# A two-layer model on one core: the first 40 up tiles of each layer get 512 moving columns, their folds set in between the routing's instructions

## The reference

```python
q = (xb @ w_q).reshape(tb, PEER_HEADS, 2, PEER_KEY_DIM)
sc = jnp.einsum('thpk,hpnk->thpn', q, sub_keys).astype(jnp.float32)
s1, i1 = lax.top_k(sc[:, :, 0], PEER_TOPK)
s2, i2 = lax.top_k(sc[:, :, 1], PEER_TOPK)
cand = (s1[..., :, None] + s2[..., None, :]).reshape(tb, PEER_HEADS, PEER_TOPK * PEER_TOPK)
cidx = (i1[..., :, None] * PEER_NKEYS + i2[..., None, :]).reshape(tb, PEER_HEADS, PEER_TOPK * PEER_TOPK)
top_s, pos = lax.top_k(cand, PEER_TOPK)
idx = jnp.take_along_axis(cidx, pos, axis=-1)
gw = jax.nn.softmax(top_s, axis=-1).astype(xb.dtype)
act = jax.nn.gelu(jnp.einsum('td,thkd->thk', xb, u[idx]), approximate=False)
return jnp.einsum('thk,thkd->td', act * gw, v[idx])
```

## Time and profile before

| | us |
|---|---|
| median of 3 executions | 1962.82 |
| lowest, highest | 1962.61, 1963.25 |
| span of the profiled execution, first to last instruction | 1961.0 |
| PE busy in the span | 1935.7 (99%) |
| DVE busy | 1186.3 (60%) |
| POOL busy | 1242.2 (63%) |
| ACT busy | 961.2 (49%) |

### The profile page before, as it was taken

The page is one execution under the profiler, slowest core; times in us unless marked ns, Lnnn a source line. Parts: engine busy times, 40 slices in busy tenths (PEclk is TensorE's granted clock), DMA queues, the critical chain, the costliest instruction groups (busy, mean ns, idle before and its releaser), DMA issues.

```text
span 1961.0 us, 39380 instructions
## 1 busy us (share of the span) xinstructions
PE 1935.7 (99%) x13126; PEld 1750.7 (89%) x13126; DVE 1186.3 (60%) x2802; ACT 961.2 (49%) x1521; POOL 1242.2 (63%) x624
## 2 busy tenths in 40 slices
PE   9999999999999999999999999999999999999998
PEld 9888899899999888888898889998999998888886
DVE  4654499368898444444456536983688974444444
ACT  5644445444444444444555544454444444444444
POOL 6446688877776555555474476888777765555553
PEclk9999999999999999999999999999999999999999
DMA  6524555554444666655545245555444445555553
GB/s 217 179 91 145 187 182 176 190 172 156 155 155 156 196 193 192 195 192 194 187 142 185 87 152 186 183 181 189 165 157 152 158 163 192 195 193 193 192 192 135
DMA packets 93245, 338.48 MB, mean 173 GB/s; under 512 B 10353, under 2 KB 10737, under 8 KB 93169
## 3 DMA queue, kind: packets, MB, share of 16 engines
q1 hardware_dynamic: 93168, 337.54, 51.4%
HBM read 336.45 MB, written 1.05 MB: 172 GB/s over the span
## 4 chain that ended last, share of the span: by engine, by line
PE 95%; DVE 2%; ACT 1%; DMA 1%; issue 0%; SPq 0%; DVEq 0%
PE PS L1011 35%; PE PS L934 11%; PE PS L935 10%; PE PS L939 10%; PE PS L896 8%; PE PS L574 6%; PE PS L901 4%; PE PS L948 3%; PE PS L835 2%; DMA ring<-stream 1%; PE PS L559 1%; PE PS L541 1%; PE PS L564 1%; PE PS L560 1%; PE PS L613 1%; PE PS L921 0%
## 5 line engine op out<-in xcount | busy, mean ns | idle before, releaser
L478 POOL TENSOR_TENSOR WL<-ring,WH 128x1024 fp32r<-128x1024 f32 x360 | 867.8, 2412 | 383.0 <-ACT WH L1265 198.4
L1265 ACT CAST WH<-ring 128x1024 fp32r<-128x1024 f32 x512 | 538.2, 1051 | 753.5 <-PE PS L1011 329.7
L508 POOL TENSOR_TENSOR HX<-G,HX 128x256 fp32r<-128x256 f32 x256 | 372.2, 1454 | 320.2 <-ACT HX L1389 320.2
L1938 DVE TENSOR_TENSOR WL<-ring,WH 128x1024 fp32r<-128x1024 f32 x248 | 303.9, 1225 | 370.9 <-ACT WH L1265 370.9
L1011 PE MATMUL PS<-WH,HX 128*128 128x512 f32 x2048 | 506.4, 389 | 0.0
L1011 PEld LDWEIGHTS PS<-WH,HX 128*128 128x128 f32 x2048 | 384.2, 188 | 80.0 <-POOL HX L508 0.5
L934 PE MATMUL PS<-HX,WH 128*128 128x256 f32 x1664 | 418.1, 289 | 0.0
L935 PE MATMUL PS<-HX,WH 128*128 128x256 f32 x1664 | 407.7, 283 | 0.0
L935 PEld LDWEIGHTS PS<-HX,WH 128*128 128x128 f32 x1664 | 319.0, 192 | 0.0
L934 PEld LDWEIGHTS PS<-HX,WH 128*128 128x128 f32 x1664 | 317.9, 191 | 0.0
L1011 PE MATMUL PS<-WL,HX 128*128 128x512 f32 x1024 | 274.0, 389 | 0.0
(11 more groups left out here) (244 smaller groups left out, 1877.6 us busy)
## 6 DMA issues: line engine op xcount, KB each, us to landing
ring<-stream SPq DMA_DIRECT2D x636, 512.0 KB, 3.3
X<-x_t SPq DMA_DIRECT2D x4, 256.0 KB, 3.6
out_t<-X SPq DMA_DIRECT2D x2, 512.0 KB, 2.7
CN<-consts SPq DMA_DIRECT2D x1, 851.0 KB, 9.4
WF<-last SPq DMA_DIRECT2D x1, 512.0 KB, 10.1
PR<-params SPq DMA_DIRECT2D x2, 239.0 KB, 4.5
CN<-consts SPq DMA_DIRECT2D x1, 64.0 KB, 4.0
```

Of the source, the lines that this page charges most:

```text
L478: nc.gpsimd.tensor_tensor(WL[:, b, :], ring[:, slot, :], WH[:, b, :].bitcast(F32), ALU.subtract).then_inc(done, 1)
L508: nc.gpsimd.tensor_tensor(GL[:, s, :], G[:, tile, :], GH[:, s, :].bitcast(F32), ALU.subtract).then_inc(L.gl_ready, 1)
L1265: nc.scalar.copy(WH[:, b, :], ring[:, slot, :]).then_inc(L.hi_ready, 1)
L1938: V.tensor_tensor(WL[:, s % 2, :], ring[:, (U0 + s) % SLOTS, :], WH[:, s % 2, :].bitcast(F32), ALU.subtract).then_inc(L.vlo_ready, 1)
```

## The change

All of the first 64 up tiles become wide. Their folds have to be done by DVE while it does the routing, so `fold` is called between the routing's instructions: `spend` adds up the columns that the instructions behind it take, plus 60 for each, and calls the next fold each time the sum passes 2100; it starts at -4500, so the first one comes after 6600. No more than 48 are set in this way, and those left of the 48 follow after the routing. ACT's gelu takes each pair two tiles later than before relative to PE, from `G`, in place. The gelu of tiles 0 and 1 ahead of the first loop is gone, so this loop holds the first gelu of the layer's up tiles. `EXP_ROUND` goes from 9 to 10, and behind the exponential one loop of six rounds takes the place of the loop of one, the four tiles written out and the loop of five. One gelu more stands after it.

```diff
-EXP_ROUND, WIDE_ROUND, TURN_ROUND = 9, 10, 12
-N_WIDE = HK - SLOTS * WIDE_ROUND
+EXP_ROUND, TURN_ROUND = 10, 12
+FOLD_LEAD, FOLD_COLUMNS, FIXED_COLUMNS = 4500, 2100, 60
...
                     def rounds_wide(lo, hi):
                         with pe.Fori(lo, hi) as r:
                             for s in range(SLOTS):
-                                pe.wait_ge(L.folded, r * SLOTS + (s - 3 - SLOTS * WIDE_ROUND))
+                                pe.wait_ge(L.folded, r * SLOTS + (s - 3))
                                 wide_in(s, r * SLOTS + (s + 1))
-                    rounds_in(1, WIDE_ROUND)
                     for s in range(SLOTS):
-                        if s >= 2:
-                            pe.wait_ge(L.gelu_done, 2 * WIDE_ROUND - 3 + s)
-                        wide_in(s, WIDE_ROUND * SLOTS + s + 1)
-                    rounds_wide(WIDE_ROUND + 1, TURN_ROUND)
+                        wide_in(s, s + 1)
+                    rounds_wide(1, TURN_ROUND)
...
-                    act.wait_ge(L.piece_done, U0 + 2)
-                    gelu(G[:, 0:2, :], 0)
+                    def gelu_wide(acts):
+                        nc.scalar.activation(acts, acts, ACT.Gelu).then_inc(L.gelu_done, 1)
                     def rounds_gelu(lo, hi):
                         with act.Fori(lo, hi) as r:
                             for s in range(SLOTS):
                                 high_r(r, s)
                                 if s == 1:
-                                    act.wait_ge(L.piece_done, r * SLOTS + U0)
-                                    gelu(G[:, bass.ds(r * SLOTS - 2, 2), :], 1)
+                                    act.wait_ge(L.folded, r * SLOTS - 2)
+                                    gelu_wide(G[:, bass.ds(r * SLOTS - 4, 2), :])
                                 if s == 3:
-                                    act.wait_ge(L.piece_done, r * SLOTS + (U0 + 2))
-                                    gelu(G[:, bass.ds(r * SLOTS, 2), :], 0)
+                                    act.wait_ge(L.folded, r * SLOTS)
+                                    gelu_wide(G[:, bass.ds(r * SLOTS - 2, 2), :])
                     rounds_gelu(1, EXP_ROUND)
                     act.wait_ge(rt_sub, TT * (layer + 1))
                     nc.scalar.activation(VC[:, :, :, :], VC[:, :, :, :], ACT.Exp).then_inc(rt_exp, 1)
-                    rounds_gelu(EXP_ROUND, WIDE_ROUND)
...
+                    rounds_gelu(EXP_ROUND, HK // SLOTS)
+                    act.wait_ge(L.folded, HK - 2)
+                    gelu_wide(G[:, HK - 4:HK - 2, :])
...
+                    folds, spent = [0], [-FOLD_LEAD]
+                    def spend(columns):
+                        spent[0] += columns + FIXED_COLUMNS
+                        if spent[0] >= FOLD_COLUMNS and folds[0] < SLOTS * TURN_ROUND:
+                            fold(folds[0])
+                            folds[0] += 1
+                            spent[0] -= FOLD_COLUMNS
                     def top16(rows, vals, idxs):
+                        n = rows[0].shape[-1]
                         for r, v in zip(rows, vals):
                             ins = V.max(v[:, 0:8], r)
                         step(ins)
+                        spend(len(rows) * (n + FIXED_COLUMNS))
                         for r, v, i in zip(rows, vals, idxs):
                             V.max_index(i[:, 0:8], v[:, 0:8], r)
                             ins = V.match_replace(r, v[:, 0:8], r, -3e38)
+                            spend(2 * n + 3 * FIXED_COLUMNS)
                         step(ins)
                         for r, v in zip(rows, vals):
                             ins = V.max(v[:, 8:16], r)
                         step(ins)
+                        spend(len(rows) * (n + FIXED_COLUMNS))
                         for r, v, i in zip(rows, vals, idxs):
                             ins = V.max_index(i[:, 8:16], v[:, 8:16], r)
+                            spend(n + FIXED_COLUMNS)
                         step(ins)
...
                         step(V.tensor_copy(v_ps, v[:, 1]))
+                        spend(3 * P)
                         step(V.tensor_tensor(CAND[t]...))
+                        spend(2048)
...
                             step(V.tensor_tensor(EQ, ...))
+                            spend(2048 + P)
                             step(V.tensor_tensor(EQ2, ...))
+                            spend(2048)
                             V.tensor_reduce(RT[:, t, e, :]...).then_inc(L.rt_ready, 1)
+                            spend(2048)
...
-                    for k in range(SLOTS * WIDE_ROUND, SLOTS * TURN_ROUND):
+                    for k in range(folds[0], SLOTS * TURN_ROUND):
                         fold(k)
```

More of the change, by code:

```diff
@@ L950, in place @@
                         mm.then_inc(L.w_done, 1)
[L952 to L960, removed]
                     def wide_in(s, ready):
@@ L988, in _ @@
                         if s % 2 == 0:
-                            pe.wait_ge(L.folded, N_WIDE - 1 + s // 2)
+                            pe.wait_ge(L.folded, HK - 1 + s // 2)
                         pe.wait_ge(L.o_ready, s + 1)
@@ L1265, in high @@
                         nc.scalar.copy(WH[:, b, :], ring[:, slot, :]).then_inc(L.hi_ready, 1)
-                    def gelu(dst, b):
-                        nc.scalar.activation(dst, bank[4 + b].rearrange("p (e n) -> p e n", e=2),
-                                             ACT.Gelu).then_inc(L.gelu_done, 1)
                     def high_k(k):
@@ L1377, in _ @@
                     high_k(HK + 1)
-                    act.wait_ge(L.folded, N_WIDE)
+                    act.wait_ge(L.folded, HK)
                     gelu_wide(G[:, HK - 2:HK, :])
```

## The result

The kernel after takes 1966.91 us (median; 1966.04 to 1967.51), the kernel before beside it on the same chip 1962.5. The ratio is 1.0022, with a 95% interval from 1.0015 to 1.0030: slower, by 4.4 us where 11.4 were forecast. The profiled span went from 1961.0 to 1965.4. In layer 0 the last wide tile starts at 413.39, in the kernel before at 411.14, so a layer loses some 2.2 us.

What follows compares the result with a forecast made beforehand. TensorE was taken to bound the up tiles, with routing 27 us early; folds and waits on VectorE would then delay tile 48 by 2.6 + 3.1 = 5.7 us a layer: 1962.8 + 11.4 = 1974.2 us, 8-in-10 range 1964 to 1982.

Steps and rivals of the forecast that it cites:

- the waits for GpSimd: VectorE's routing instructions wait for GpSimd 6.3 us a layer, hidden before, now on the path; table loads add 3.1.
- The first trio: Copy, product and tensor_scalar behind a candidate selection: 3.6 us more waiting for GpSimd, bounds 0 and 7.2.
- The wide period: Up tiles on TensorE go from 2.880 to 2.793 us each, 3.5 us a layer, 7.0 in all.
- The count of folds: Folds falling into VectorE's routing: 43 by booked columns, 37 of them before the second `rt_sub`.
- The second trio: The later copy, product and tensor_scalar on VectorE meet an idle GpSimd, saving the 0.5 us waited before.
- The clock: A stall ahead of tile 40 could lower TensorE's granted clock; nothing was booked for it.
- the stall of the exponential: Ahead of tile 40, which comes at 349.1 instead of 342.65; said to lie inside the routing's delay, adding nothing.
- Gelu: ScalarE's gelu one pair later waits for an older fold, which takes away waits; booked at nothing.
- Loads only at the loops' entry: Rival: no table loads inside rounds, GpSimd keeps gaps, VectorE's waits stay 6.3 us; 1968 us, chance 0.24.
- VectorE keeps up: Rival: waits for GpSimd go; 1960.7 us (0.10), or 1955.9 (0.05) if folds are cheaper and the exponential timely.
- Loads that stall TensorE each round: Rival: ScalarE's table loads make TensorE stall in every round; some 1990 us, chance 0.04.
- The trio waits fully: Rival: full waits for GpSimd and folds nearer 0.69 us, twice 2.4 to 3.4 us more; 1979 to 1981, chance 0.15.

Runs made afterwards that it cites:

- e5: The kernel after with a one-column exponential and gelu ahead of each round's second cast, forcing a table load behind the cast's waits: 1966.33 us.
- n1_free_waits: The kernel after with every routing instruction that had waited for GpSimd given an operand or its result in PSUM: 1959.50 us, ratio 0.9984.
- e2_psum: The kernel after with the reciprocal of the softmax's sum written to PSUM, so the last products have one SBUF input: 1963.56 us, ratio 1.0005.
- e3_exp11_psum: The kernel after with the exponential ahead of round 11 instead of 10 and the softmax reciprocal in PSUM: 1968.43 us, ratio 1.0028.
- e4_gelu: The kernel after with a one-column gelu ahead of each of the two gelu loops, so they are entered with its table: 1969.87 us, ratio 1.0034.
- e1_exp11: The kernel after with the exponential ahead of round 11 instead of round 10: 1975.24 us, ratio 1.0063.
- n6: n1_free_waits with each of a layer's first four folds done twice, the extra result going to an unused slot: 1964.17 us, ratio 1.0009.
- n5: n1_free_waits with the exponential behind the cast of tile 40, in a loop of one round of its own: 1955.79 us, ratio 0.9964.
- n3: The kernel before the change with the rewritten PSUM instructions of n1_free_waits: 1962.87 us, ratio 1.0001.

## Why the prediction was right in its direction and wrong in its size

**What failed** is the step "the waits for GpSimd": "without a gap each of them can wait a whole 2.41 us ... I take one and a half GpSimd instructions, 3.6 us". +3.1 us a layer were booked and +0.4 measured. The first trio waited 1.74 us where 3.6 were booked, and the first tensor_scalar for the lower index (L1827), booked at the 1.0 of before, waited for nothing. Two links of the step broke. The first is the load's place, ahead of the cast's wait for TensorE instead of behind it. The second is more basic: e5 puts a load behind the wait, GpSimd runs without a gap for most of a round, and the waits stay at 6.6. The two things that do set them are whether GpSimd happens to work when such an instruction comes, and for how long yet. Waits a layer and time of the kernel after and those built on it:

| kernel | waits for GpSimd, us a layer | time, us |
|---|---|---|
| n1_free_waits | 0 | 1959.50 |
| e2_psum | 2.9 | 1963.56 |
| e5_load_behind_the_wait | 6.6 | 1966.33 |
| after | 6.7 | 1966.91 |
| e3_exp11_psum | 6.1 | 1968.43 |
| e4_gelu | 8.6 | 1969.87 |
| e1_exp11 | 9.8 | 1975.24 |

Only e3 is out of order: its waits come together, two of 2.2 us in 11 us, and tiles 41 and 44 wait for folds (1.66 and 1.56 us). The sum is not the price: from tile 0 to the last wide tile n1 takes 178.51 us and the kernel after 182.28, 3.8 us for 6.7 us of waits, since the two stalls lie partly inside each other. Whether a certain instruction meets GpSimd at work depends on small shifts, 0.14 us in e1 and 0.39 us in e4. I know no way to forecast that from the profile of before; the honest term was 6.3 with bounds on both sides, and taking a middle value with a reason attached made it look firmer than it was.

**A smaller term.** A fold was booked at 0.61 net. (366.82 - 227.92 - 113.67 - 0.4) / 43 gives 0.577, 1.4 us a layer less, and n6's doubled folds give 0.58. With the routing's start 0.2 us later, the sum runs: forecast 370.7 for the routing's end, less 2.7, less 1.4, plus 0.2, is 366.8; it ended at 366.90.

**What held.** The wide period: n5, where nothing holds TensorE, gives (407.49 - 230.76 - 0.58) / 63 = 2.796 us a tile with the transposes taken off, and 1955.79 us in all, where the prediction had 1955.9 for a TensorE unheld. The count of folds, 43 and 37. That VectorE's chain sets the end: e2 for the fold ahead of tile 47, n6 for the exponential. The way from the routing's end over a fold and tile 47 to tile 48: 366.90 to 371.10, 4.2 us, against 371.7 - 367.6 = 4.1. The second trio on an idle GpSimd. The clock only in layer 0; in layer 1 it fell behind tile 40's stall, and that no time was lost by it was luck, as the fold ahead of tile 47 was late anyway. That the stall of the exponential lies inside the other: e2 took the routing's away, gained 3.4 us, and the other stall stayed as it was. The load without a further drain: 343.14 + 1.29 is the cast at 344.43, so the drain that the Trainium skill, ScalarE: Activation LUTs, section "What ACT_TABLE_LOAD costs", adds to a load does not show in this kernel.

**A small error.** Gelu was booked at nothing. It waits for folds that VectorE is behind with, and here its own table load comes behind that wait, not in spare time; the next casts queue behind both (the row at 324.27 is followed by two casts at 324.81):

```profile
322.98 1.28 ACT L1299 ACT_TABLE_LOAD   x1 [2.05 <-DVE G L1759]
324.27 0.63 ACT L1299 ACTIVATE G<-G  x1
...
367.63 0.63 ACT L1299 ACTIVATE G<-G  x1 [4.23 <-DVE G L1759]
```

Tiles 34, 35 and 39 are 0.65 us late in sum, which the stall of tile 40 covers, and tile 49 is 0.3 us later than in n1, which nothing covers.

**The rivals.** "Loads only at the loops' entry" gave 1968, near the result, with waits of 6.3, but by a cause that did not occur: the loads come in every round. It was the right size of the waits. "VectorE keeps up" did not come true in the kernel after, but its working did in experiments: all waits gone was worth 1960.7 by it and 1959.50 in n1. Loads that stall TensorE each round did not show. "The trio waits fully" comes nearest in e1, where the waits are 9.8 us.

**Left open.** The exponential's new place without the edits of n1 wasn't tried, so how much of n5's gain stands without them isn't known. The waits give the sign of the 3 us between e4 and the kernel after, and by the wait ahead of the exponential about the size (tile 40 is 1.96 us later); the shifts behind it were not followed back. What decides whether the clock falls behind a stall isn't known either: the same stall of 1.8 us ahead of tile 40 left it at 1.00 in layer 0 of the kernel after and in both layers of e2, e5 and n6. Each trace is of one execution.

## What to carry to other kernels

Work that is put between the instructions of another engine's free time also brings onto the path every wait that had been hidden there: count these first, they were 6.3 us a layer here against 3.5 us to be gained. Waits by chance overlap move by several us with any shift, so remove them (here by an operand or a result in PSUM, which cost no measurable time in n3) before other edits are judged; e1's move lost 8 us with them and nothing without. A rare function on ScalarE went best directly behind an instruction that was on time and ahead of one that needed no load after it (n5, the only run that tried it). A profile of one layer is not enough: the other had a stretch at half the clock.

## What the runs showed of the hardware that had not been expected

- A load of ScalarE's tables can come ahead of a wait of the instruction that needs it: ahead of the cast's wait for TensorE (load 237.15, cast 238.83) and of the exponential's wait for VectorE (load 339.94, instruction 342.70). It does not pass every wait: the gelu's load came behind its wait for a fold (322.98, after 2.05 us idle). What makes the difference was not tested.
- A stall of TensorE of 1.77 us was followed by a granted clock of 0.50 in layer 1 of the kernel after and in both layers of e4 (there 1.87 us), and not in layer 0 of the kernel after. In e1 a stall of 1.99 us was followed by it in layer 1, one of 1.98 us in layer 0 was not. So the length of the stall alone does not decide it.
- Behind the exponential a cast needs no load (n5, 341.87), while at a loop's entry it got one (after, 343.14).
- VectorE's instructions with an operand or result in PSUM never waited for GpSimd, in n1 all ten of a layer. The Trainium skill, SBUF — State Buffer, section "SBUF: two separate sides", names the exclusive port pair for two SBUF inputs or a two-port mode, and this agrees. A result in PSUM made the tensor_scalar 0.06 us longer (0.28 against 0.22), against waits of up to 2.2 us.
- Once one of them has waited for GpSimd, its companions can get through if GpSimd has a gap then: the copy ended at 301.16 and two more were done by 301.63, in a gap of 0.48 us.
